# Strassen's seven products in the two feed-forward stages of a streaming encoder step, with the weight sums on GpSimd

## The chip, the cores and the metric

The kernel runs on one NeuronCore of a Trainium2 chip. TensorE (PE) multiplies matrices out of SBUF into PSUM; VectorE (DVE), ScalarE (ACT) and GpSimd (POOL) work elementwise, and GpSimd reaches SBUF alone; SyncE (SP) issues nearly all DMAs. The metric is the device time in microseconds of one execution, the median of several runs. Everything is in float32; lower is better.

## The reference, cut to what matters

Two layers are run over 1152 tokens (1024 of a prompt, 8 x 16 of samples) with a width of 1024. Each layer has a mixer and then the feed-forward stage that the change is about; 2816 is the stage's inner width:

```python
def conv_ffn(h, conv_hist, w_in, conv_w, conv_b, w_out):
    """(gelu(causal_dwconv(x W_a)) * x W_b) W_down."""
    T = h.shape[1]
    proj = jnp.einsum('btd,df->btf', h, w_in)              # 1024 -> 2 * 2816
    a, gate = proj[..., :D_FF], proj[..., D_FF:]
    full = jnp.concatenate([conv_hist.astype(a.dtype), a], axis=1)
    conv = conv_b + sum(full[:, j:j + T] * conv_w[j] for j in range(CONV_W))   # CONV_W = 3
    y = jnp.einsum('btf,fd->btd', jax.nn.gelu(conv, approximate=False) * gate, w_out)   # 2816 -> 1024
    return y, full[:, -(CONV_W - 1):].astype(conv_hist.dtype)

# per layer: x = x + mixer(rms_norm(x)); x = x + conv_ffn(rms_norm(x)); at the end y = rms_norm(x)
```

## The kernel before, in words

Activations lie transposed in SBUF: the width on the partitions (8 blocks of 128), the tokens along the free side. PE's fast float32 form rounds its operands, so every operand is kept in two parts, a high one (a rounded copy by ACT) and a low one (the remainder, a subtraction by DVE), and each product is three matmuls: high x high, high x low, low x high. In the names, `wh`/`wl` are the parts of a weight piece of 128x512, `xh`/`xl` of the activations, `yh`/`yl` of the inner activations.

A feed-forward stage goes in 11 steps over the inner width. In a step four units (`unit`, L707; its matmul is L723) make 2 x 128 inner channels of `a` and of the gate, each unit from 8 blocks of the width, 3 parts and 3 token blocks of 384: 72 matmuls of 128x384. DVE scales the result out of PSUM (L1417) and does the convolution (L1888 to L1900), ACT the gelu (L2610), GpSimd the product with the gate and its low part (L2977, L2983). Then `down` (L733, matmul L748, L772 for the last steps of layer 0) multiplies by 256 rows of `w_out`: 144 matmuls, which DVE adds to the residual `xs` (L1424). PE needs a step's inner activations only one step later, so its stream is never broken. The gain of the norm is multiplied into the weights by GpSimd (L2836), and 1/rms is applied when a result leaves PSUM. So a stage begins with activations that are not yet normed, while the norm is still being worked out: the squares by ACT, their sum by GpSimd (L2842), the sum over partitions by PE (L790), the root by ACT (L2215), the reciprocal by DVE (L1436).

Layer 0's stage is followed by the projection of the chunk mixer (`v` groups, L1246, 128x512 matmuls with the activations as the stationary operand). Layer 1's last two down steps are fused with the final norm and the output (`fin_part`, L1335, matmul L1353): PE turns the residual into rows beside them, so that only the last tile's norm and store come after the last matmul.

The order of the work is written out by hand, engine by engine, with semaphores between them; a table of counts (`PLAN`) numbers the weight pieces and the uses of the accumulator banks. One DMA queue (SP) loads the weights, 256 KB a piece, four pieces ahead.

## Time and profile before

| | us |
|---|---|
| median of 3 runs | 2838.18 |
| lowest and highest run | 2835.65, 2838.43 |
| the profiled execution: span from its first to its last instruction | 2835.0 |
| span less than the median | 3.2 |
| feed-forward stage of layer 0, to the first `v` matmul | 830.5 |
| feed-forward stage of layer 1, to the end | 845.2 |

The profile gives for each engine the time in which it was busy, the chain of work that ended last, and groups of instructions with their mean duration. A matmul's own duration overlaps that of the next; the spacing of a row of them is what counts. The stages are told apart by the line of their matmuls.

### The profile page before, as it was taken

The numbers are of one execution on the slowest core, as the hardware profiler recorded it, in microseconds if no ns is written. First come the engines' busy times: TensorE is split into PE (matmuls) and PEld (weight loads), VectorE is DVE, ScalarE is ACT, GpSimd is POOL, SyncE is SP. The second block draws the span as 40 slices with busy tenths as digits, with TensorE's granted clock in tenths as the row PEclk, the third lists the DMA queues.
The fourth block names the chain that finished last, engine by engine and source line by source line (L and its number), as shares of the span: only waits on it lengthen the run. The fifth ranks groups of instructions, "written<-read, shape, count | busy, mean of one in ns | idle before, by whom it ended". The sixth has DMA issues, their size and how long they took to land.

```text
span 2835.0 us, 44317 instructions
## 1 busy us (share of the span) xinstructions
PE 2809.9 (99%) x16164; PEld 2735.6 (96%) x16164; DVE 1477.7 (52%) x2678; ACT 707.6 (25%) x1191; POOL 733.5 (26%) x540
## 2 busy tenths in 40 slices
PE   9999999999999999999999999999999999999999
PEld 9999999999999999999888999999999999999997
DVE  3658975554444444457323755556544444444454
ACT  4424463211111111114222221214211111111114
POOL 3233325322222222223001230013422222222220
PEclk9999999999999999999999999999999999999999
DMA  4111001111111111111211111111111111111112
GB/s 146 41 43 40 24 27 48 41 42 41 44 41 41 42 43 41 41 45 45 60 51 58 34 42 41 44 41 34 52 42 41 44 41 41 44 41 41 44 48 85
DMA packets 195026, 130.70 MB, mean 46 GB/s; under 512 B 8876, under 2 KB 186741, under 8 KB 194677
## 3 DMA queue, kind: packets, MB, share of 16 engines
q1 hardware_dynamic: 194900, 129.43, 15.2%
q8 instruction: 61, 1.00, 0.1%
q14 instruction: 33, 0.26, 0.0%
q10 hardware_dynamic: 32, 0.01, 0.0%
HBM read 120.60 MB, written 8.81 MB: 46 GB/s over the span
## 4 chain that ended last, share of the span: by engine, by line
PE 94%; DVE 4%; issue 1%; ACT 1%; DMA 0%; POOL 0%; DVEq 0%; SPq 0%; ACTq 0%; POOLq 0%
PE bank L723 49%; PE bank L748 21%; PE bank L1246 7%; PE bank L772 3%; PE bank L884 3%; PE bank L1170 2%; PE bank L1353 2%; PE bank L919 1%; PE bank L822 1%; PE bank L1306 1%; DVE qsc L1548 1%; DVE work L2050 0%; PE bank L1138 0%; DVE sct L1569 0%; PE bank L905 0%
## 5 line engine op out<-in xcount | busy, mean ns | idle before, releaser
L2836 POOL TENSOR_TENSOR raw<-raw,vec 128x512 f32<-128x512 f32 x248 | 279.5, 1138 | 1297.2 <-DMA raw<-in_w_in_ffn 844.3
L723 PE MATMUL bank<-xh,wh 128*128 128x384 f32 x2664 | 607.2, 335 | 0.7 <-issue 0.7
L723 PE MATMUL bank<-xl,wh 128*128 128x384 f32 x2664 | 604.5, 334 | 0.0
L723 PE MATMUL bank<-xh,wl 128*128 128x384 f32 x2664 | 604.4, 334 | 0.0
L2181 ACT ACTIVATE wh<-raw 128x512 fp32r<-128x512 f32 x374 | 235.3, 629 | 1396.3 <-PE bank L723 781.1
L1398 DVE TENSOR_TENSOR wl<-raw,wh 128x512 fp32r<-128x512 f32 x374 | 283.7, 759 | 424.9 <-ACT wh L2181 424.9
L723 PEld LDWEIGHTS bank<-xh,wh 128*128 128x128 f32 x2664 | 473.6, 188 | 2.8 <-issue 1.5
L723 PEld LDWEIGHTS bank<-xl,wh 128*128 128x128 f32 x2664 | 474.6, 188 | 0.0
L723 PEld LDWEIGHTS bank<-xh,wl 128*128 128x128 f32 x2664 | 474.4, 188 | 0.0
L1424 DVE TENSOR_TENSOR xs<-bank,xs 128x384 f32<-128x384 f32 (+1 forms) x648 | 320.9, 550 | 280.3 <-PE bank L748 246.8
L748 PE MATMUL bank<-yh,wh 128*128 128x384 f32 x1152 | 265.0, 338 | 0.0
L748 PE MATMUL bank<-yl,wh 128*128 128x384 f32 x1152 | 264.9, 338 | 0.0
L748 PE MATMUL bank<-yh,wl 128*128 128x384 f32 x1152 | 264.8, 338 | 0.0
L748 PEld LDWEIGHTS bank<-yh,wl 128*128 128x128 f32 x1152 | 207.4, 188 | 0.0
L748 PEld LDWEIGHTS bank<-yh,wh 128*128 128x128 f32 x1152 | 207.3, 188 | 0.0
L748 PEld LDWEIGHTS bank<-yl,wh 128*128 128x128 f32 x1152 | 207.2, 188 | 0.0
L2977 POOL TENSOR_TENSOR gate<-gate,cv 128x1152 f32<-128x1152 f32 x40 | 115.5, 2887 | 233.5 <-DVE xs L1424 211.7
L1417 DVE TENSOR_TENSOR gate<-bank,rstd 128x384 f32<-128x384 f32 x132 | 65.4, 550 | 178.9 <-PE bank L723 178.9
L1417 DVE TENSOR_TENSOR apad<-bank,rstd 128x384 f32<-128x384 f32 x88 | 45.0, 553 | 137.4 <-PE bank L723 137.4
L2983 POOL TENSOR_TENSOR yl<-gate,yh 128x1152 fp32r<-128x1152 f32 x40 | 114.7, 2885 | 0.0
L2610 ACT ACTIVATE cv<-cv 128x1152 f32<-128x1152 f32 x44 | 51.4, 1168 | 248.3 <-DVE cv L1895 248.3
L1892 DVE SCALAR_TENSOR_TENSOR cv<-apad,convc,cv 128x1024 f32<-128x1024 f32 x88 | 112.2, 1275 | 0.0
(340 smaller groups left out, 3369.6 us busy)
## 6 DMA issues: line engine op xcount, KB each, us to landing
raw<-in_w_in_ffn SPq DMA_DIRECT2D x176, 256.0 KB, 2.9
raw<-in_w_out_ffn SPq DMA_DIRECT2D x88, 256.0 KB, 2.7
raw<-in_w_uv_c SPq DMA_DIRECT2D x64, 256.0 KB, 2.8
raw<-in_w_in_ab SPq DMA_DIRECT2D x40, 256.0 KB, 2.9
raw<-in_w_out_c SPq DMA_DIRECT2D x32, 256.0 KB, 2.7
xtok<-in_x_prompt SPq DMA_DIRECT2D x8, 512.0 KB, 7.7
raw<-in_w_out_ab SPq DMA_DIRECT2D x16, 256.0 KB, 2.7
out_y_prompt<-otok SPq DMA_DIRECT2D x8, 512.0 KB, 2.6
```

The lines of the kernel that those rows point to most:

```text
L723: mm = pe.matmul(ps[(sg + tb) % BANKS][:, 0:TB], w[:, place, k * P:(k + 1) * P], r[:, kk, tbs(tb)], start=kk == 0 and c == 0, stop=kk == K ...
L748: mm = pe.matmul(ps[(sg + g0 + tb) % BANKS][:, 0:TB], w[:, place, k * 256 + dd * P:k * 256 + (dd + 1) * P], r[:, k, tbs(tb)], start=k == 0 ...
L772: mm = pe.matmul(ps[(g0 + tb) % BANKS][:, 0:TB], w[:, a, k * 256 + dd * P:k * 256 + (dd + 1) * P], r[:, k, tbs(tb)], start=first, stop=last)
L1246: mm = pe.matmul(ps[g % BANKS][:, :], x[:, k, t * P:(t + 1) * P], w, start=k == 0 and e == 0, stop=k == KD - 1 and e == 2)
L1398: dve.tensor_tensor(wl[:, s % 2, :], raw[:, s % RAWS, :], wh[:, s % 2, :].bitcast(F32), ALU.subtract)\
L1417: dve.tensor_tensor(dst, ps[bank % BANKS][:, 0:TB], rstd[:, tbs(tb)], ALU.mult)\
L1424: dve.tensor_tensor(xs[:, d, tbs(tb)], ps[sg % BANKS][:, 0:TB], xs[:, d, tbs(tb)], ALU.add)\
L1892: dve.scalar_tensor_tensor(outp, padp[:, j:j + SEQ], col(16 + j), outp, ALU.mult, ALU.add)\
L2181: act.activation(wh[:, s % 2, :], raw[:, s % RAWS, :], ACT.Copy).then_inc(w_high_ready, 1)
L2836: pool.tensor_tensor(r, r, g, ALU.mult).then_inc(w_scaled, 1)
L2977: pool.tensor_tensor(gate[:, c, :], gate[:, c, :], cv[:, c, :], ALU.mult)\
L2983: pool.tensor_tensor(yl[:, c, :], gate[:, c, :], yh[:, c, :].bitcast(F32), ALU.subtract)\
```

## The change

Both feed-forward stages are written anew; the rest is touched only where the stages meet it.

Each of the two multiplications is seen as two by two blocks times two by two blocks: the width in halves of 512, the inner channels in pairs of 128-blocks (up) or the output width in halves (down), the tokens in halves of 576. Strassen's scheme makes the four result blocks from seven block products, not eight, each of a sum of weight blocks and a sum of activation blocks; the results are added up afterwards. Every operand still has a high and a low part.

**Up.** 22 pairs of 128-blocks, 7 products each. A product is 4 blocks of the half width x 3 parts x 2 chunks of 288 tokens: 24 matmuls of 128x288 (L1391 in the new file), into one double bank. The activations are normed first, in place (`normed`, by DVE), and the seven sums of them are formed once in a stage (`combos`) and kept with their parts in 28 tiles of 2 x 576. The four sums of weights of a pair are formed by GpSimd (`first_sums`, `up_sum`) from unscaled weights. ACT and DVE take each product out of PSUM and combine it with saved ones (`up_evict`).

**Room.** The 28 tiles need the room of the residual and of the inner activations. So the residual `xs` goes to a scratch tensor in DRAM before it is normed, and comes back in the down part; the inner activations `y` are stored to DRAM too, 2 blocks a step, and are read back in four blocks.

**Down.** 7 products of 11 steps; a step is 4 output blocks x 3 parts x 2 chunks: 24 matmuls (L1423) again. GpSimd forms the sums of weights (`w_sum`, 5 of the 7 products) and of `y` (`y_sum`, 5 of the 7, of which 3 are the same); parts lie in rings of 4 steps. The first two and the last two steps of a product are run as pairs, output block by output block. After each product DVE adds its four results to the residual (`down_evict`).

**Ends.** The stage of layer 0 ends with the high and low parts of the new residual, which the `v` groups wait for (`finished`, after the last step). The fused end of layer 1 is gone: after the last step PE turns the tiles, then square, root, reciprocal, product with the gain and store follow per tile (`finish`).

```diff
@@ the plan
-    PLAN.add(f"f{_l}0", 8, 12, 16)
-    PLAN.add(f"f{_l}", 9 * 12, 9 * 36, 9 * 40)
-    PLAN.add(f"f{_l}u", 8, 12, 16)
+HT = TOK // 2
+CH = HT // 2
+PAIRS = 2 * STEPS
+UPS = 7 * PAIRS
+DOWNS = 7 * STEPS
+RING = 3
+RINGD = 4
+        UP_ORDER = (1, 6, 2, 7, 5, 4, 3)
+        DOWN_ORDER = (2, 1, 5, 3, 6, 4, 7)
+        SUMMED_W, SUMMED_Y = (2, 1, 5, 6, 7), (1, 3, 6, 4, 7)
@@ SP
+                for d in range(KD):
+                    sp.wait_ge(acc_free, g0 + NTB * (d + 1))
+                    sp.dma_start(xscr[l][d], xs[:, d, :]).then_inc(x_moved, 16)
...
+                store_y(STEPS - 1)
+                step_weights(8)
+                sp.wait_ge(y_saved[0], 16 * 12 * (l + 1))
+                y_tiles(yb22[:, 9:11, :], 20, 22, T2S, y_back[2])
+                for d in range(0, KD, 4):
+                    sp.dma_start(xs[:, d:d + 4, :], xscr[l][d:d + 4].rearrange("d p t -> p d t")).then_inc(x_moved, 16)
@@ PE
+                def product(n, j):
...
+                    pe.wait_ge(f_high, done + pos + 1)
+                    pe.wait_ge(f_low, done + pos + 1)
...
+                    for k in range(4):
+                        if n == 0:
+                            pe.wait_ge(c_high, (28 + DOWNS) * l + 4 * j + k + 1)
+                            pe.wait_ge(c_low, (28 + DOWNS) * l + 4 * j + k + 1)
+                        x, _, m = combo(j, k)
+                        for e, (w, part) in enumerate(((fh, 0), (fh, 1), (fl, 0))):
+                            for c in range(2):
+                                mm = pe.matmul(bank[:, M0 + c * CH:M0 + (c + 1) * CH], w[:, pos % RING, k * P:(k + 1) * P],
+                                               x[:, m, part, c * CH:(c + 1) * CH], start=first and k == 0 and e == 0,
+                                               stop=k == 3 and e == 2, skip_group_check=True)
+                    mm.then_inc(f_done, 1)
...
+                for j in range(7):
+                    r0 = STEPS * j
+                    for first, last in ((0, 2), *((k, k + 1) for k in range(2, STEPS - 2)), (STEPS - 2, STEPS)):
+                        for f in range(4):
+                            for kk in range(first, last):
+                                down_step(r0 + kk, f)
@@ DVE, the start of a stage
+                for pos in range(RING):
+                    up_low(pos)
+                inv_rms(1 + 2 * l)
+                dve.wait_ge(x_moved, 160 * l + 16 * KD)
+                for d in range(4):
+                    normed(d, T1S)
+                for k in range(4):
+                    combo_low(0, k)
+                for k in range(4):
+                    normed(k, T2S)
+                    normed(4 + k, T2S)
+                    normed(4 + k, T1S)
+                    combos(k)
+                    combo_low(1, k)
...
+                for pos in range(1, UPS):
+                    if 2 <= pos < 7:
+                        for k in range(4):
+                            combo_low(pos, k)
+                    up_evict(pos - 1)
+                    convs(pos)
+                    if pos + 2 < UPS:
+                        up_low(pos + 2)
@@ GpSimd, the down part
+                def w_sum(r):
...
+                    pool.wait_ge(raw_loaded[ra], va)
+                    pool.wait_ge(raw_loaded[rb], vb)
+                    ring_free(r)
+                    pool.tensor_tensor(ring(r)[2], fraw[:, ra, :], fraw[:, rb, :],
+                                      ALU.subtract if q in (6, 7) else ALU.add).then_inc(f_summed, 1)
...
+                    pool.wait_ge(f_done, done + UPS + r - 3)
+                    pool.tensor_tensor(yslf[:, r % RINGD, :], y_block(a, kk), y_block(b, kk),
+                                       ALU.subtract if q in (3, 4) else ALU.add).then_inc(ys_summed, 1)
...
+                for r in range(4, DOWNS):
+                    w_sum(r)
+                    y_sum(r)
+                    j, kk = divmod(r, STEPS)
+                    if l == 0 and j == 6 and 4 <= kk <= 9:
+                        for m in (2 * kk - 8, 2 * kk - 7):
+                            add_square(24 * 2 + m, m % 2, m % NTB, sq_b, ssq_b)
@@ ACT, the end of layer 0's stage
+            def finished(d):
+                act.wait_ge(d_out, 24 + d + 1 if d < 4 else 20 + d - 3)
+                act.activation(xh[:, d, :], xs[:, d, :], ACT.Copy).then_inc(xh_ready, NTB)
```

DVE at the start of the first feed-forward stage: before, three low parts of weights and the reciprocals, then at once the scaling of results (`apad`, `cv` are the convolution's tiles).

```order
L1860 MEMSET apad 128x2 x2
L1398 TENSOR_TENSOR wl<-raw,wh 128x512 x3
L1436 RECIPROCAL rstd<-rstd 128x384 x3
L1417 TENSOR_TENSOR apad<-bank,rstd 128x384 x2
L1870 TENSOR_TENSOR apad<-bank,rstd 128x256
L1871 TENSOR_TENSOR apad<-bank,rstd 128x8x16
L1875 TENSOR_SCALAR apad<-convc 128x8x2
```

And in the changed kernel, behind the same reciprocals, the last of four such blocks and what comes next (`cw`, `cx` hold the activation sums, `fl` low parts of weights, `u_`, `p_` saved products).

```order
L2011 SCALAR_TENSOR_TENSOR xs<-xs,vec,rstd 128x576 x3
L2022 TENSOR_TENSOR cxf<-xs 128x576
L2024 TENSOR_TENSOR cxf<-xs 128x576
L2026 TENSOR_TENSOR cwf<-xs,cxf 128x576
L2029 TENSOR_TENSOR cxf<-xs,cwf 128x576
L2038 TENSOR_TENSOR cw<-cwf,cw 128x576
L2172 MEMSET apad_a 128x2
L2173 MEMSET apad_b 128x2
L2008 TENSOR_TENSOR fl<-flf,fh 128x512
L2038 TENSOR_TENSOR cw<-xs,cw 128x576 x4
L2053 TENSOR_TENSOR u_100<-bank,p_102 128x576
```

Norming and 16 sums now stand on DVE ahead of the second product's operands.

GpSimd around the end of the first feed-forward stage, before: gate product and low part, then the last weights to scale, then the squares' sums.

```order
L2836 TENSOR_TENSOR raw<-raw,vec 128x512 x3
L2977 TENSOR_TENSOR gate<-gate,cv 128x1152 x2
L2983 TENSOR_TENSOR yl<-gate,yh 128x1152 x2
L2836 TENSOR_TENSOR raw<-raw,vec 128x512 x5
L3010 MEMSET ssq_b 128x1152
L2842 TENSOR_TENSOR ssq_b<-ssq_b,sq_b 128x384 x24
```

And in the changed kernel's down part, product 6 of the first stage (`flf` sums of weights, `yslf` sums of `y`).

```order
L3281 TENSOR_TENSOR flf_113<-fraw 128x512
L3311 TENSOR_TENSOR yslf<-yb_119,yb_121 128x576
L3281 TENSOR_TENSOR flf<-fraw 128x512
L3311 TENSOR_TENSOR yslf<-yb_119,yb_121 128x576
L3281 TENSOR_TENSOR flf<-fraw 128x512
```

Each step of such a product now has two sums on GpSimd in front of its ACT and DVE parts.

## Rows read from the trace of the kernel before

**Rows 1.** The page: span, then engines' busy time.

```profile
span 2835.0 us, 44317 instructions
PE 2809.9 (99%) x16164; PEld 2735.6 (96%) x16164; DVE 1477.7 (52%) x2678; ACT 707.6 (25%) x1191; POOL 733.5 (26%) x540
```

**Rows 2.** The chain of waits: start us, us, what.

```profile
509.26 12.49 PE bank L723 x72
...
612.22 25.35 PE bank L748 x144
637.56 49.92 PE bank L723 x288
...
1481.16 65.33 PE bank L1246 x288
...
1989.78 6.24 PE bank L723 x36
```

**Rows 3.** Timeline of PE at layer 0's end: start us, us, engine, line, what.

```profile
1339.78 0.39 PE L1246 MATMUL bank<-wh,xh 128*128 128x512 f32 x1
```

**Rows 4.** Chain of waits after it.

```profile
1361.60 38.57 PE bank L1246 x170
```

**Rows 5.** Timeline of DVE in a step.

```profile
651.68 0.68 DVE L1398 TENSOR_TENSOR wl<-raw,wh 128x512 fp32r<-128x512 f32 x1
652.29 0.80 DVE L1888 TENSOR_SCALAR cv<-apad,convc 128x1024 f32<-128x1024 f32 x1
...
653.27 1.27 DVE L1892 SCALAR_TENSOR_TENSOR cv<-apad,convc,cv 128x1024 f32<-128x1024 f32 x1
654.47 0.34 DVE L1895 SCALAR_TENSOR_TENSOR cv<-apad,convc,cv 128x128 f32<-128x128 f32 x1
```

**Rows 6.** Timeline, layer 0's last down steps; brackets: idle before, and its releaser.

```profile
1299.71 0.55 DVE L1424 TENSOR_TENSOR xs<-bank,xs 128x384 f32<-128x384 f32 x1
1300.17 1.49 DVE L1430 TENSOR_TENSOR xl<-xs,xh 128x384 fp32r<-128x384 f32 x3
1301.31 7.77 POOL L2842 TENSOR_TENSOR ssq_b<-ssq_b,sq_b 128x384 f32<-128x384 f32 x6 [41.23 <-ACT sq_b L2208]
...
1304.26 3.96 DVE L1430 TENSOR_TENSOR xl<-xs,xh 128x384 fp32r<-128x384 f32 x3
```

**Rows 7.** Timeline of GpSimd: products and sums of 1152 and 512 columns.

```profile
635.74 2.69 POOL L2977 TENSOR_TENSOR gate<-gate,cv 128x1152 f32<-128x1152 f32 x1 [11.35 <-DVE xs L1424]
...
1573.13 5.16 POOL L3048 TENSOR_TENSOR gbc<-gbc,bbc 128x512 f32<-128x512 f32 x4
```

**Rows 8.** Timeline of the first stage's start.

```profile
509.15 1.49 DVE L1424 TENSOR_TENSOR xs<-bank,xs 128x384 f32 x3 [1.49 <-PE bank L1170]
510.87 3.68 POOL L2842 TENSOR_TENSOR ssq_e<-ssq_e,sq_e 128x384 f32<-128x384 f32 x3 [2.34 <-ACT sq_e L2208]
525.28 0.58 ACT L2215 ACTIVATE rstd<-bank,vec 128x384 f32<-128x384 f32 x1 [1.63 <-PE bank L790]
523.12 7.37 DVE L1436 RECIPROCAL rstd<-rstd 128x384 f32<-128x384 f32 x3
```

**Rows 9.** Instructions grouped by line: ACT copies, 512 and 1152 wide.

```profile
L2181 ACT ACTIVATE wh<-raw 128x512 fp32r<-128x512 f32 x374 | 235.3, 629 | 1396.3 <-PE bank L723 781.1 <-PE bank L748 524.8 <-PE bank L1170 34.4
L2606 ACT ACTIVATE yh<-gate 128x1152 fp32r<-128x1152 f32 x44 | 51.4, 1168 | 57.4 <-POOL gate L2977 51.8 <-DVE gate L1908 5.5
```

**Rows 10.** By stretch: us, busy (count) per engine, PEclk, DMA share, GB/s.

```profile
0.00:20.00 20.00, 15.07 (x75) 14.00 (x76) 7.71 (x14) 9.22 (x20) 11.54 (x28) 1.00 0.93 316
160.00:164.00 4.00, 4.00 (x17) 4.00 (x17) 0.00 (x0) 0.38 (x1) 2.97 (x3) 0.57 0.00 0
```

**Rows 11.** Timeline of the last tile.

```profile
2827.33 1.05 PE L1362 MATMUL bank<-ident,xs 128*128 128x128 f32 x8
...
2829.81 0.60 ACT L2803 ACTIVATE fin_sq<-bank 128x512 f32<-128x512 f32 x1 [2.65 <-PE bank L1353]
...
2831.12 1.41 DVE L2170 SCALAR_TENSOR_TENSOR otok<-bank,fin_sums,fin_gain 128x512 f32<-128x512 f32 x2
```

**Rows 12.** The page: DMA issues, KB each, us to landing.

```profile
raw<-in_w_out_ffn SPq DMA_DIRECT2D x88, 256.0 KB, 2.7
out_y_prompt<-otok SPq DMA_DIRECT2D x8, 512.0 KB, 2.6
```

More of the change, by code:

```diff
@@ new lines, in build, with up_slot, formed, combo @@
+        LOADS0 = tuple(STEPS * sum(len(DOWN_LOADS[q]) for q in DOWN_ORDER[:j]) for j in range(7))
+        def up_slot(n, q):
+            return psp[(3 * n + UP_SLOT[q]) % 4]
+        def formed(l, k, which):
+            return 32 * l + 4 + 7 * k + which + 1
+        def combo(x, k):
+            m = 4 * x + k
+            return (cw, cwf, m) if m < 12 else (cx, cxf, m - 12)
+        FFN_LOADS = STEPS + (LOADS0[6] + 2 * STEPS + 7) // 8
+        def loads_before(l, s):
+            return (PIECES if l else V_N) // RAWS + FFN_LOADS * l if s < RAWS else (FFN_LOADS - 1) * l
@@ new lines, in ring, with y_block, up_sums, sums_of @@
+        def ring(r):
+            e = (3, 1, 2, 0)[r % 4]
+            return (fh3[:, :], fl3[:, :], flf3[:, :]) if e == 3 else (fh[:, e, :], fl[:, e, :], flf[:, e, :])
+        def y_block(b, kk):
+            if b == 21 and kk == STEPS - 1:
+                return yb21_last[:, :]
+            return {11: yb11, 12: yb12, 21: yb21, 22: yb22}[b][:, kk, :]
+        def up_sums(l, n, which):
+            return (4 * PAIRS + len(SUMMED_W) * STEPS) * l + 4 * n + which + 1
+        def sums_of(r, which):
+            j, kk = divmod(r, STEPS)
+            return STEPS * sum(q in which for q in DOWN_ORDER[:j]) + kk + 1
@@ new lines, in build, with on_dve, on_act, dest @@
+        U2, U3, C22, C21, C12 = range(5)
+        P1, C11 = range(2)
+        def on_dve(l, n, which):
+            return 5 * (PAIRS * l + n) + which + 1
+        def on_act(l, n, which):
+            return 2 * (PAIRS * l + n) + which + 1
+        def dest(n, c, h):
+            if n % 2:
+                return ((gate[:, c, (T1S, T2S)[h]], slice(0, HT)),)
+            padp, pads = pads_of(c)
+            if h == 0:
+                return ((padp[:, 2:2 + HT], slice(0, HT)),)
+            return ((padp[:, 2 + HT:2 + SEQ], slice(0, SEQ - HT)), (pads[:, :, 2:], slice(SEQ - HT, HT)))
@@ L1393, in _ @@
+            for t in range(NT):
+                finish(t)
         @block.vector
@@ L1815, in abo @@
                         low(n0 + 4 * i + 2 * u + 1, n0 + 2 * u + 1)
-                    if not first or u:
+                    if (not first or u) and not (last and u):
                         low(n0 + 4 * i + 2 * u + 2, n0 + 2 * u + 2)
@@ L2461, in gate_silu @@
                 act.wait_ge(acc_free, g0 + 3 * (16 + h) + 3)
-                act.activation(work[:, 12 + h, :], work[:, 12 + h, :], ACT.Silu).then_inc(g_act, 1)
+                act.activation(work[:, 12 + h, :], work[:, 12 + h, :], ACT.Silu).then_inc(q_act, 1)
             def head_high(h):
@@ L2554, in _, with abo @@
             n0, g0, t0 = PLAN.at["abo"]
-            def abo(i):
-                first = isinstance(i, int)
+            def abo(i, first=False, last=False):
                 for u in range(2):
-                    if not first or u:
+                    if (not first or u) and not (last and u):
                         for p, tk in ((2, 1), (3, 4)):
@@ new lines, in ffn @@
+                for pos in range(RING):
+                    up_high(pos)
+                rms(1 + 2 * l)
+                for x in range(2):
+                    for k in range(4):
+                        combo_high(x, k)
+                act.wait_ge(convc_mm, 1 + l)
+                act.activation(convc[:, :], ps[7][:, 0:440], ACT.Copy).then_inc(convc_ready, 1)
+                for pos in range(1, UPS):
+                    n, j = divmod(pos, 7)
+                    if pos < 6:
+                        for k in range(4):
+                            combo_high(pos + 1, k)
+                    up_evict(pos - 1)
+                    if pos + 2 < UPS:
+                        up_high(pos + 2)
+                    else:
+                        w_high(pos + 2 - UPS)
+                        y_high(pos + 2 - UPS)
+                    if n % 2 and j == 5:
+                        gelu(n // 2, 0)
+                    if n % 2 == 0 and n and j == 2:
+                        gelu(n // 2 - 1, 1)
@@ L3002, in ffn @@
[L3002 to L3016 removed]
+                done = PER * l
@@ new lines, in ffn @@
+                if l == 0:
+                    pool.wait_ge(states_stored, 16 * (1 + HEADS))
+                up_sum(1)
+                for pos in range(3, UPS):
+                    up_sum(pos)
+                    n, j = divmod(pos - 2, 7)
+                    if n and n % 2 == 0 and j in (0, 4):
+                        y_prod(n // 2 - 1, j // 4)
+                w_sum(0)
+                w_sum(1)
+                y_prod(STEPS - 1, 0)
+                w_sum(2)
+                w_sum(3)
+                y_prod(STEPS - 1, 1)
```

1222 lines of the change are left out of this document (671 added, 551 removed).

## The prediction

> **What bounds the kernel now.** I read the page's shares first: PE is busy for 2809.9 of 2835.0 us, the others for half of it or less [rows 1]. The chain of waits then shows two patterns that alternate through both feed-forward stages: 288 matmuls of a step's four units in 49.92 us and 144 of its down part in 25.35 us [rows 2], one behind the other without a gap. That is 173.3 and 176.0 ns per matmul of 384 columns. Nothing but PE bounds these stages, so fewer or shorter matmuls are worth their whole time, until another engine can no longer keep up. Fewer columns go through PE after the change (7 of 8 products), but the other engines get much more to do, so the question is where PE will wait.
>
> Stage of layer 0: from 509.26 [rows 2] to the first `v` matmul at 1339.78 [rows 3], 830.5 us. Stage of layer 1: from 1989.78 [rows 2] to 2835.0, 845.2 us.
>
> **PE's part.** No row has a stream of matmuls of 288 columns. The `v` groups' 288 matmuls of 512 columns take 65.33 us [rows 2], 226.8 ns each; against 173.3 for 384 columns that is 53.5 ns for 128 columns, 0.418 ns a column, with 13.3 ns fixed. So 288 columns: 120.4 + 13.3 = 133.7 ns, with the ends 120 (nothing fixed) and 173.3 (no shorter than 384). I take 133.5, a product or a down step of 24 is 3.20 us, and 3.23 with what a change of group costs. A layer has 22 x 7 = 154 products and 7 x 11 = 77 down steps: 231 x 3.23 = 746 us. By PE alone the change would save 84 us in layer 0 and 99 in layer 1.
>
> **A stage's start.** Before, PE begins at once on activations that are not normed; now all 28 activation sums wait for the norm. Before the first product: the last residual sums (1.49), squares, their sums on GpSimd (3.68 for three), the root (0.58), the reciprocals (7.37) [rows 8]; some overlap, about 13 us. `normed` also waits for the residual's eight stores of 590 KB to the scratch tensor: 4.7 MB at the 316 GB/s of the kernel's fastest stretch [rows 10] is 15 us, started while the norm is worked out, so it hides nearly all of itself. Then DVE norms 16 tiles (8 blocks in two halves), forms 16 sums and takes 28 low parts, 60 operations of 576 columns. A DVE operation with two inputs takes 0.61 us for 512 columns and 1.20 for 1024, from one start to the next [rows 5]: 0.68 for 576. With 0.73 for the norming ones, 42 us; the evictions, `fl` parts and first copies among them add 6, and PE at a lower clock after its pause 2 to 3 (such a stretch exists: PEclk 0.57 with short, scattered matmuls [rows 10]). ACT's 28 copies of 576 columns lie between 629 and 1168 ns each [rows 9], 0.68 by their width, 19 us in all, beside DVE. Pair 0 ends about 64 us after the stage's start; its PE work is 7 x 3.23 = 22.6. Loss: 41 us a layer. Bounds: 28 (the stores, evictions and half the norm hidden) and 50 (sums slowed by GpSimd).
>
> **The up part.** For 14 products (two pairs, 45.2 us on PE) GpSimd has 8 weight sums of 512 columns and two gate products of 1152. It takes 5.16/4 = 1.29 us for 512 and 2.69 for 1152 columns [rows 7]; 8 x 1.2 + 2 x 2.69 = 15 us. DVE has some 25: evictions, low parts, two convolutions at about 4.3. Even if they excluded each other the 40 us fit under 45.2, so I let the remaining 147 products go at PE's pace: 475 us. If this cover fails by a tenth, it costs 20 us or more a layer.
>
> **Up to down.** The last convolution, gate product, high and low part and the first sums follow one another: 4.3 + 2.7 + 1.2 + 2.4 us and PE has two pairs' products of margin for a part of it only. I take 11 us, bounds 2 and 18.
>
> **The down part.** 77 x 3.23 = 249 us. In products 1, 6 and 7 (33 steps) GpSimd forms both a weight sum (512) and a `y` sum (576), and DVE takes the low part of each. What these cost together stands in the rows of the squares' sums: alone, three DVE low parts of 384 columns take 1.49 us; beside six GpSimd sums in 7.77 us, 3.96 us for three [rows 6]. One of each then takes 7.77/6 to 3.96/3, 1.30 to 1.32 us, where one DVE operation alone takes 0.50 and a GpSimd one 0.90 (2.69 us x 384/1152, [rows 7]): nearly their sum, so they exclude each other. 1.32/384 is 3.44 ns a column; 1088 columns give 3.74 us a step against PE's 3.23. 33 x 0.51 = 17 us a layer. Ends: 0 (they overlap; GpSimd's 1088 columns alone are 2.6 us) and 50 (each waits for the other's hand-over too). The rings are four steps deep, which covers a step or two, not eleven. The other four products have one such sum or none and stay under 3.23.
>
> The Trainium skill ("SBUF — State Buffer", the section on SBUF's two separate sides) says that GpSimd and VectorE share a port pair that one holds for a whole instruction, and that only VectorE operations with two SBUF inputs or a fast copy mode need it. [Rows 6] agree: the low parts, with two SBUF inputs, are held up, and L1424's sum out of PSUM takes its 0.55. By that rule the evictions here would go free, as I assume.
>
> **Small stalls.** Evictions between products, and SP's queue: the residual's return (4.7 MB, 15 us by [rows 10]) and `y`'s reads stand in front of weight pieces that otherwise land in 2.7 us [rows 12]. 8 us a layer, between 0 and 25.
>
> **Only in layer 0.** Twelve squares' sums stand in GpSimd's product 7, 0.9 us each as above: 10 us where GpSimd and DVE are already the limit. Then `v`. Before, it begins inside the stage and runs without gaps from 1361.60 [rows 4], 21.8 us after its first matmul. Now `xh`, `xl` and the squares of the last four blocks all follow the last steps: four evictions, copies and low parts at 2 us a block, six squares' sums at 1.1, norm and reciprocals as before. 36 us; 14 lost (bounds 5 and 25).
>
> **Only in layer 1.** After the last step: an eviction (0.68), eight transposes (1.05), squares (two of 0.60), root and reciprocal, the product with the gain (1.41) [rows 11], a store (2.6, [rows 12]) make 8 us with the hand-overs; eight more tiles share two output buffers: (1.41 + 2.6)/2 = 2.0 each. 24 us.
>
> **Sum.** 64 + 475 + 11 + 249 + 17 + 8 = 824, less 1 of rounding up: 823. Layer 0: 823 + 10 = 833, + 14 at `v`, against 830.5: +16. Layer 1: 823 + 24 = 847 against 845.2: +1.5. The span becomes 2835.0 + 17.5 = 2852.5; the median lies 3.2 above the span, so 2855 us.
>
> **Rivals.**
>
> A, the forecast: 0.55. Its own range is 2830 to 2880.
>
> B, GpSimd and DVE don't hold each other up in the down part as they do in [rows 6] (there a chain through two buffers of squares could have set the pace as well). Then the 34 us of heavy steps, the 10 of squares and some 10 of the hand-overs come back: 2801 us. For it: GpSimd alone needs 2.6 of 3.23 us. Against it: the low part's 0.50 became 1.32 beside running GpSimd work, which no buffer explains. 0.27.
>
> C, it comes out clearly slower by one mechanism: in products 1, 6 and 7 sum, copy and low part pass from GpSimd to ACT and DVE, and the ring's release comes back from PE three or four steps later. If exclusion and these waits add up to 4.5 us a step, 66 steps lose another 0.76 each, 50 us: 2905. It decides from about 3.9 us a step upwards. 0.11.
>
> D, PE's waits in these steps lower its clock. [Rows 10] show 0.57 of full speed in a stretch of scattered matmuls. At 1.2 GHz a step's 24 x 120 ns double; four fifths of that, 2.3 us in 66 steps, make 152 us: 3007. Against it: a wait here is a fraction of a microsecond between dense steps, not such a stretch. 0.04.
>
> E, the shorter matmul isn't cheaper: at 173.3 ns as for 384 columns, 11,088 matmuls x 40 ns = 443 us, about 3300. 0.03. [Rows 2] speak against it, since 512 to 384 columns follows a line nearly through zero.
>
> The Trainium skill ("TensorE: Matmul & The Clock Gate", Part 3, on the mechanism) lets a weight load overlap a running matmul only in another row group; by its 107 ns for a load, estimated, a matmul would take 120 + 107 = 227 ns and the change cost a millisecond more. [Rows 2] refute it for this kernel: 384 columns are 160 ns of columns and come every 173.3.
>
> **Numbers.** Two executions of this kernel can't be told apart below about 0.2%, here 2832.5 to 2843.9. Of A, 0.05 lies below, 0.12 within, 0.38 above. Faster: 0.05 + 0.27 = 0.32; same 0.12; slower 0.38 + 0.11 + 0.04 + 0.03 = 0.56. For 8 in 10 the range takes in B almost wholly and half of C: 2785 to 2905, with about 0.05 left below and 0.13 above.
>
> **What would show it.** The spacing of the new matmuls (133 ns; 3.23 us a product). The first product 13 to 17 us after the stage's start and pair 0's end at 64. In the down part 3.7 us a step in products 1, 6, 7 and 3.23 in the others, with DVE's low parts and GpSimd's sums never beside each other at full speed. A pause of about 11 us between up and down, `v` undisturbed 36 us after the last step, 24 us behind the last matmul. I am wrong if the up part runs slower than PE (DVE or GpSimd over 3.2 us a product), if the start costs 50 or more, or if the heavy steps run at 3.23.

## The result, and the profile after

The changed kernel takes 2871.6 us (median of 4 runs, 2869.6 to 2874.2) against 2837.5 of before (4 runs): ratio 1.0122, 95% interval 1.0108 to 1.0137. It is slower by 34 us. The forecast was slower, 2855 us; the direction was right and the size half of it. Its profiled span is 2867.9 us, 32.9 more than before's.

The page of the changed kernel: its span, then busy time by engine, as in [rows 1], and the clock in 40 slices.

```profile
span 2867.9 us, 45432 instructions
...
PE 2682.9 (94%) x17812; PEld 2595.6 (91%) x17812; DVE 1882.1 (66%) x2649; ACT 932.6 (33%) x1536; POOL 1056.8 (37%) x724
...
PEclk9999999699999998999999999999699999998999
```

PE's busy time fell by 127 us, and 127 + 33 = 160 us more of the span are now idle. DVE gained 404 us of work and GpSimd 323.

The long undisturbed stretch answers to [rows 2]. The chain of waits, layer 1's up part:

```profile
2082.30 467.82 PE bank L1391 x3528
```

467.82 / 3528 is 132.6 ns for a matmul of 288 columns; 133.5 was forecast from the line through 384 and 512 columns. Apart from pair 0 the up part runs at PE's pace without a gap, in both layers.

The two stages, term by term. "Measured" is read from the timeline of PE: the starts of every 24th matmul of L1391 and L1423 (264 make a down product).

| term, us | predicted | layer 0 | layer 1 |
|---|---|---|---|
| start of stage to the end of pair 0 | 64 | 72.9 | 73.2 |
| the other 147 products | 475 | 467.6 | 467.6 |
| pause between up and down | 11 | 7.0 | 7.0 |
| 77 down steps at PE's pace | 249 | 244.3 | 244.3 |
| lost in products 1, 6, 7 (two sums a step) | 17 | 16.6 | 16.6 |
| lost in product 2 (and the rest) | 8 | 18.3 | 21.8 |
| squares' sums in product 7 | 10 | 13.0 | |
| **to the last down matmul** | 833 / 823 | **839.7** | **830.5** |
| entry of `v`, or tail | 36 / 24 | 37.2 | 25.1 |

Before, the stages were 830.5 + 21.8 (entry of `v`) and 845.2, so these lines are 24.6 and 10.4 us more; 2 us less elsewhere make up the 32.9. Two lines of the table are a split and not a reading: layer 0's product 7 lost 16.7 us as a whole; 3.7 of it, as much as in layer 1, stand under the two sums a step, the other 13.0 under the squares' sums.

Stretches of the changed kernel: start of layer 0's stage, pair 0, the rest of the up part, product 2, product 1. Columns as in [rows 10].

```profile
507.00:528.00 21.00, 5.07 (x10) 1.91 (x8) 14.64 (x15) 7.43 (x13) 5.97 (x5) 0.59 0.51 180
528.00:554.00 26.00, 10.14 (x47) 9.03 (x48) 25.19 (x37) 3.96 (x7) 2.28 (x1) 0.63 0.00 0
554.00:580.00 26.00, 19.93 (x124) 18.58 (x124) 22.90 (x31) 15.19 (x27) 5.12 (x3) 0.85 0.14 42
580.00:1045.00 465.00, 465.00 (x3511) 464.23 (x3510) 336.11 (x463) 141.44 (x211) 182.51 (x104) 1.00 0.24 74
...
1055.00:1108.00 53.00, 40.81 (x266) 39.96 (x267) 28.87 (x32) 14.83 (x27) 21.78 (x13) 0.82 0.94 345
1108.00:1148.00 40.00, 36.92 (x261) 36.00 (x260) 37.44 (x30) 14.29 (x22) 34.23 (x21) 0.96 0.61 205
```

Four kinds of stretch read differently. In pair 0 DVE is busy for 48.1 of 52 us (third pair of numbers) while PE is busy for 30 (first pair); from 580 on PE is full and DVE at 72%; in product 2 the last two numbers stand out, the DMA engines at 94% and 345 GB/s; in product 1 DVE and GpSimd are both near full, 37.4 and 34.2 of 40 us.

What PE waited for in the down part of layer 0: the first matmul behind a wait, in brackets how long and on what.

```profile
1096.70 0.82 PE L1423 MATMUL bank<-ysh,fh 128*128 128x288 f32 x2 [10.37 <-ACT fh L2874]
1100.25 0.82 PE L1423 MATMUL bank<-ysh,fh 128*128 128x288 f32 x2 [1.77 <-ACT fh L2874]
...
1137.68 0.50 PE L1423 MATMUL bank<-ysh,fh 128*128 128x288 f32 x2 [0.18 <-ACT fh L2874]
1141.24 0.50 PE L1423 MATMUL bank<-ysh,fh 128*128 128x288 f32 x2 [2.52 <-ACT fh L2874]
```

The 10.4 us stand before step 9 (13.8 in layer 1); the prediction had 8 us for all small stalls together. The 2.5 us at the end of product 1 stand inside the two-step pair. By the order of the work it needs both its steps' parts, and so takes the slack of the ring at once; no run changes this order.

The waits are not the whole loss. Behind the 2.5 us the matmuls come in twos every 0.48 us, not every 0.27, and the granted clock is 0.50, the lower of TensorE's two levels (timeline, then a stretch with columns as in [rows 10]):

```profile
1143.10 0.68 PE L1423 MATMUL bank<-ysh,fl 128*128 128x288 f32 x2
1143.58 0.68 PE L1423 MATMUL bank<-ysh,fh 128*128 128x288 f32 x2
...
1142.20:1145.40 3.20, 3.20 (x15) 3.20 (x15) 3.20 (x6) 1.20 (x2) 0.03 (x1) 0.50 1.02 365
```

So product 1's 5.7 us are 3.1 of waits, 1.9 of slower matmuls and some smaller delays; product 6's 7.2 are 3.2 and 3.3. Of product 2's 17.9 us in layer 0, 5.2 are slower matmuls, behind the pause between up and down and behind the one before step 9; of product 7's 16.7 there, 5.0 are (0.6 in layer 1).

GpSimd in such steps (layer 1, product 1), and DVE beside it:

```profile
2641.96 1.94 POOL L3311 TENSOR_TENSOR yslf<-yb,yb 128x576 f32<-128x576 f32 x1
2643.86 1.73 POOL L3281 TENSOR_TENSOR flf<-fraw 128x512 f32<-128x512 f32 x1
2645.55 1.93 POOL L3311 TENSOR_TENSOR yslf<-yb,yb 128x576 f32<-128x576 f32 x1
```

```profile
2642.69 1.75 DVE L2125 TENSOR_TENSOR fl<-flf,fh 128x512 fp32r<-128x512 f32 x1
2644.64 1.56 DVE L2133 TENSOR_TENSOR ysl<-yslf,ysh 128x576 fp32r<-128x576 f32 x1 [0.20 <-ACT ysh L2892]
```

A sum follows a sum without a pause: 3.59 us a step (2641.96 to 2645.55), against PE's 3.18. The prediction had 3.74. Each DVE operation takes more than twice the 0.69 and 0.75 us that it takes alone.

### The profile page after: what moved, and what is told of

Read it like the earlier page. It is cut to its first block, busy times and chain, and to the rows that moved or that the text cites. A ratio compares the mean times of both kernels' runs of the same rounds, so it can differ in the third digit from the quotient of the medians.

```text
span 2867.9 us, 45432 instructions
## 1 busy us (share of the span) xinstructions
PE 2682.9 (94%) x17812; PEld 2595.6 (91%) x17812; DVE 1882.1 (66%) x2649; ACT 932.6 (33%) x1536; POOL 1056.8 (37%) x724
## 4 chain that ended last, share of the span: by engine, by line
PE 43%; POOL 3%; issue 2%; DVE 2%; DMA 1%; SPq 1%; ACT 0%; POOLq 0%; DVEq 0%; ACTq 0%
PE bank L1391 16%; PE bank L889 7%; PE bank L1459 6%; PE bank L914 5%; PE bank L1423 5%; PE bank L938 2%; POOL yslf L3311 1%; POOL flf L3281 1%; PE bank L1518 1%; DVE work L2284 0%; DMA y_scratch<-gate 0%; SPq L758 0%; DMA out_y_prompt<-otok 0%; DMA fraw<-in_w_out_ffn 0%; DVE otok L2392 0%
## 5 line engine op out<-in xcount | busy, mean ns | idle before, releaser
L1391 PE MATMUL bank<-cx,fh 128*128 128x288 f32 x2816 | 487.3, 294 | 7.0 <-DVE cx L2038 6.2
L1391 PE MATMUL bank<-cw,fh 128*128 128x288 f32 x2112 | 375.4, 300 | 56.3 <-DVE cw L2038 36.8
L1391 PEld LDWEIGHTS bank<-cx,fh 128*128 128x128 f32 x2816 | 411.8, 188 | 9.1 <-issue 8.0
L1391 PEld LDWEIGHTS bank<-cw,fh 128*128 128x128 f32 x2112 | 315.6, 192 | 62.7 <-issue 34.2
L1423 PE MATMUL bank<-ysh,fh 128*128 128x288 f32 x1232 | 275.8, 306 | 54.0 <-ACT fh L2874 35.6
L1391 PE MATMUL bank<-cx,fl 128*128 128x288 f32 x1408 | 298.8, 294 | 0.0
L1423 PE MATMUL bank<-ysh,fl 128*128 128x288 f32 x1232 | 271.2, 302 | 0.0
L1423 PE MATMUL bank<-ysl,fh 128*128 128x288 f32 x1232 | 270.3, 302 | 0.0
L1423 PEld LDWEIGHTS bank<-ysh,fh 128*128 128x128 f32 x1232 | 204.7, 196 | 63.4 <-ACT fh L2874 41.4
L1391 PE MATMUL bank<-cw,fl 128*128 128x288 f32 x1056 | 227.7, 298 | 0.0
L1391 PEld LDWEIGHTS bank<-cx,fl 128*128 128x128 f32 x1408 | 224.6, 187 | 0.0
L1423 PEld LDWEIGHTS bank<-ysl,fh 128*128 128x128 f32 x1232 | 205.6, 196 | 0.0
L1423 PEld LDWEIGHTS bank<-ysh,fl 128*128 128x128 f32 x1232 | 204.9, 195 | 0.0
L1391 PEld LDWEIGHTS bank<-cw,fl 128*128 128x128 f32 x1056 | 172.1, 191 | 0.0
```

What stands on the lines that cost most here:

```text
L1391: mm = pe.matmul(bank[:, M0 + c * CH:M0 + (c + 1) * CH], w[:, pos % RING, k * P:(k + 1) * P], x[:, m, part, c * CH:(c + 1) * CH], start=fi ...
L1423: mm = pe.matmul(psp[f][:, M0 + c * CH:M0 + (c + 1) * CH], w[:, f * P:(f + 1) * P], x[:, r % RINGD, c * CH:(c + 1) * CH], start=kk == 0 an ...
```

## The experiments

All are timed against the kernel before; ratios are to it, with their 95% interval, and the changed kernel stands at 1.0122. The first question was whether the pace of the heavy steps is set by exclusion (GpSimd and DVE on SBUF) or by the hand-over through ACT and the ring; the second, what bounds product 2; the third, whether the start is DVE's row of operations.

### e1: weights before the wait in SP's queue

```diff
-                step_weights(8)
+                for r in range(8, 12):
+                    step_weights(r)
                 sp.wait_ge(y_saved[0], 16 * 12 * (l + 1))
                 ...
-                for r in range(9, DOWNS):
+                for r in range(12, DOWNS):
```

> SP issues the weights of down steps 9 to 11 before it waits for the last inner activations to be stored, and before the residual's return. Theory (the one queue's order: step 9's weights stand behind a wait for a store, behind the rest of y, the residual and the conv tails): the pause of 10.4 us in layer 0 and 13.8 us in layer 1 before step 9's matmuls goes, and with it most of the 17.7 and 21.2 us that product 2 loses; 28 to 36 us in all, about 2840 us. Rival (the bytes are what takes the time, not their order: 4.7 MB of the residual and y come in one way or another): under 10 us, the pause moves to step 11 or to the first product's additions.

Measured: 2855.5 us, 1.0072 [1.0055, 1.0088], 16 us less than the change. Product 2 takes 45.8 and 47.4 us instead of 52.8 and 56.3. Neither side had the size. The pause before step 9 went, as the theory said, but as the rival said PE now waits at the first additions, which need the residual: 8.1 us, and 9.4 in layer 1. PE of this kernel, step 11:

```profile
1100.82 0.82 PE L1424 MATMUL bank<-ysh,fh 128*128 128x288 f32 x2 [8.12 <-DVE xs L2154]
```

### e5: half of the residual earlier

Product 2's additions need blocks 4 to 7 only, and their room is free during the up part.

```diff
                 step_weights(1)
+                sp.dma_start(xs[:, 4:8, :], xscr[l][4:8].rearrange("d p t -> p d t")).then_inc(x_half, 16)
...
-                for d in range(0, KD, 4):
-                    sp.dma_start(xs[:, d:d + 4, :], ...).then_inc(x_moved, 16)
+                sp.dma_start(xs[:, 0:4, :], ...).then_inc(x_moved, 16)
```

> As e1_queue, and the half of the residual that product 2's additions need (blocks 4 to 7, whose place is free) comes back already before the down part, the other half where it came before. After e1_queue product 2 still lost 10.7 and 12.3 us, of which PE waited 8.1 and 9.4 us for the first additions, and these for the residual. Theory (the residual's return is what is late): product 2 falls to 37 us or less in both layers, 16 us less than e1_queue, about 2840. Rival (the queue is short of time as a whole: what is brought earlier makes y or weights late): the pause moves to product 1 or before step 3, under 6 us gained.

Measured: 2848.3 us, 1.0044 [1.0030, 1.0058]; product 2 41.2 and 42.6 us. The median is 7 us under e1's and the profiled span 13; the intervals just meet, and the products' times show the 4.6 and 4.8 us gained here. That is less than expected but no shift: PE's wait for the first additions fell from 8.1 to 3.5 us (from 9.4 to 4.9 in layer 1). Together e1 and e5 take back about 12 of the 18 and 14 of the 21 us.

### e9: fewer bytes in product 2

Built on e8 (below). In e1 and e5 the DMA engines were busy for all of product 2, so I took bytes to be the floor. That stretch of e1 and of e5 (columns as in [rows 10]):

```profile
1055.00:1101.00 46.00, 37.79 (x265) 37.29 (x266) 24.90 (x28) 15.87 (x29) 23.87 (x14) 0.91 1.02 382
```

```profile
1056.00:1097.00 41.00, 37.68 (x264) 37.15 (x264) 23.75 (x27) 15.68 (x28) 23.70 (x14) 0.93 0.99 363
```

```diff
+                        n = 128 if 4 <= r < 12 else 512
-                        sp.dma_start(fraw[:, s, :]..., wfo[l][:, k:k + 1, fhalf * 512:(fhalf + 1) * 512])
+                        sp.dma_start(fraw[:, s, 0:n]..., wfo[l][:, k:k + 1, fhalf * 512:fhalf * 512 + n])
```

> e8_all with the weight pieces of down steps 4 to 11 loaded to 128 of their 512 columns (leaves out the rest of these loads: 3.1 MB a layer). In e8_all the DMA engines are busy for the whole of product 2, at 362 GB/s, and it takes 41.7 and 43.7 us instead of 35.1. Theory (product 2 is bound by bytes, after the order in the queue was mended): 3.1 MB at 362 GB/s are 8.7 us, so product 2 falls to 37 or 38 us in both layers, 8 to 11 us in all, about 2798. Rival (what is left are waits in the order of the work: the tails' way through ACT, the two-step pairs, the first additions): under 3 us.

Measured: 2804.0 us, 0.9884 [0.9867, 0.9900], beside 2810.0, 0.9901 [0.9884, 0.9918], of e8 on the same chip. The medians are 6 us apart and the intervals overlap. Product 2 took 40.7 and 42.5 us instead of 40.8 and 44.1, 1.7 us in all where 8 to 11 were expected; the other 4 us lie outside it and I can't assign them. The theory fell: once the order is mended, bytes no longer bound this product. Its stretches show what does (same columns):

```profile
1055.00:1060.00 5.00, 4.99 (x24) 4.44 (x23) 1.30 (x3) 0.45 (x1) 4.84 (x2) 0.65 0.70 196
1060.00:1065.00 5.00, 3.03 (x13) 3.03 (x13) 3.09 (x4) 2.94 (x8) 1.27 (x2) 0.69 0.76 236
1065.00:1070.00 5.00, 5.00 (x38) 5.00 (x38) 1.70 (x3) 2.32 (x4) 2.54 (x2) 0.96 1.03 372
1070.00:1090.00 20.00, 20.00 (x153) 20.00 (x152) 10.67 (x16) 7.44 (x13) 8.01 (x5) 1.00 0.70 254
```

In the timeline of PE the matmuls behind the pause between up and down, and again behind a wait of 2.0 us for the tails' bank, come in twos every 0.48 us, then every 0.27:

```profile
1061.97 0.85 PE L1427 MATMUL bank<-ysh,fh 128*128 128x288 f32 x2 [1.97 <-ACT trow L2833]
...
1064.06 0.68 PE L1427 MATMUL bank<-ysl,fh 128*128 128x288 f32 x2
1064.54 0.68 PE L1427 MATMUL bank<-ysh,fl 128*128 128x288 f32 x2
...
1065.97 0.43 PE L1427 MATMUL bank<-ysh,fh 128*128 128x288 f32 x2
1066.24 0.43 PE L1427 MATMUL bank<-ysl,fh 128*128 128x288 f32 x2
```

The granted clock there is 0.65 and 0.69, the lower of TensorE's two levels for part of the stretch. 2.0 us of waiting and 27 matmuls that together come 3.6 us late are 5.5 of the 5.8 us that layer 0's product 2 still loses. Layer 1's loses 7.6: 2.0 us at the same bank, 3.7 in slow matmuls, and 1.6 at the first additions, which wait for DVE:

```profile
2568.18 0.50 PE L1427 MATMUL bank<-ysh,fh 128*128 128x288 f32 x2 [1.57 <-DVE xs L2187]
```

### e2: all sums of the heavy steps on DVE

```diff
+                def dve_sums(r):
+                    ...
+                    dve.wait_ge(f_done, done + UPS + r - 3)
+                    if q in SUMMED_W: dve.tensor_tensor(ring(r)[2], fraw[:, ra, :], fraw[:, rb, :], ...)
+                    if q in SUMMED_Y: dve.tensor_tensor(yslf[:, r % RINGD, :], y_block(a, kk), y_block(b, kk), ...)
...
+                        dve_sums(r + 1)
                     w_low(r)
                     y_low(r)
```

> From the second down product on, DVE forms the sums of weights and of y, not GpSimd. Theory (GpSimd and DVE exclude each other; a step with two sums is 3.6 us of GpSimd time beside 3.19 of PE): DVE does two sums and two low parts in 2.55 us a step, with the evictions 33 of 35 us a product, so the waits of products 1, 6 and 7 (5.5, 7.0, 3.5 us a layer) nearly go; product 7 of layer 0, with the squares' sums still on GpSimd, falls from 51.4 to about 44 us. 32 to 40 us in all, about 2835. Rival (the hand-over from sum to high part to low part and the ring of four set the pace): no gain, or slower, since DVE now waits for PE twice a step: 2870 or more.

Measured: 2831.9 us, 0.9984 [0.9974, 0.9993]: 40 us less than the change, and just under the kernel before. Product 1 takes 34.9 us in both layers (40.6), product 6 35.7 (42.1), product 7 35.8 in layer 1 (38.6) and 42.7 in layer 0 (51.6). DVE in product 1:

```profile
1127.97 0.69 DVE L2149 TENSOR_TENSOR flf<-fraw 128x512 f32<-128x512 f32 x1 [0.54 <-PE bank L1423]
1128.58 0.75 DVE L2161 TENSOR_TENSOR yslf<-yb,yb 128x576 f32<-128x576 f32 x1
1129.25 0.69 DVE L2125 TENSOR_TENSOR fl<-flf,fh 128x512 fp32r<-128x512 f32 x1
1129.85 0.75 DVE L2133 TENSOR_TENSOR ysl<-yslf,ysh 128x576 fp32r<-128x576 f32 x1
```

Four operations in 2.6 us, where two of them took 3.3 beside GpSimd. DVE has twice the operations and is done sooner, and now even waits for PE.

### e3: no sums of weights, sums of y left on GpSimd

This takes work away and leaves the path from GpSimd to ACT to DVE and back from PE as it was.

```diff
-        SUMMED_W, SUMMED_Y = (2, 1, 5, 6, 7), (1, 3, 6, 4, 7)
+        SUMMED_W, SUMMED_Y = (2,), (1, 3, 6, 4, 7)
```

> Leaves out the sums of weights from the second down product on (the first of the two pieces is used as it is; both are loaded); the sums of y stay on GpSimd. Theory (exclusion): 1.43 us of GpSimd and 1.27 of DVE a step are 2.7, under PE's 3.19, so the waits of products 1, 6 and 7 go and layer 0's product 7 comes to 40 us or less: 35 to 43 us, about 2832. Rival (hand-over and ring: the y sum still goes from GpSimd to ACT to DVE and comes free by PE): the waits stay, under 10 us gained.

Measured: 2834.1 us, 0.9992 [0.9983, 1.0002]; products 1 and 6 34.9 us, product 7 42.2 and 35.1 (40 or less was expected of layer 0's, where the squares' sums are still on GpSimd). With e2 this settles it: the waits go when the sum of both engines' durations comes under PE's step, whether the sums of `y` stay on GpSimd (e3) or all go to DVE (e2). The way through ACT and the ring of four are there in both.

### e4: narrow norm

```diff
+                    few = slice(ts.start, ts.start + 32)
-                    dve.scalar_tensor_tensor(xs[:, d, ts], xs[:, d, ts], ..., rstd[:, ts], ALU.mult, ALU.mult)
+                    dve.scalar_tensor_tensor(xs[:, d, few], xs[:, d, few], ..., rstd[:, few], ALU.mult, ALU.mult)
```

> Norms 32 columns of each tile instead of 576 (leaves out the rest of the norm's product), 16 operations a layer. Theory (at a stage's start PE waits for DVE's row of operations and for nothing else, so each of them counts in full): 16 x 0.65 = 10.4 us a layer, 21 us in all, about 2851. Rival (ACT's copies, the weight sums on GpSimd or the scratch stores of the residual come next close behind): under 8 us in all.

Measured: 2853.0 us, 1.0062 [1.0046, 1.0079], 19 us less. From the stage's start to pair 0's end it is 64.4 us instead of 72.9 in layer 0, 65.4 instead of 73.2 in layer 1: 8.5 and 7.8 of the 10.4 us taken out.

### e11: narrow reciprocals

Built on e8.

```diff
+                    few = slice(tb * TB, tb * TB + (16 if k in (1, 3) else TB))
-                    dve.reciprocal(rstd[:, tbs(tb)], rstd[:, tbs(tb)]).then_inc(rstd_ready, 1)
+                    dve.reciprocal(rstd[:, few], rstd[:, few]).then_inc(rstd_ready, 1)
```

> e8_all with the reciprocals at the start of both stages taken over 16 of each 384 columns (leaves out the rest). Theory (the chain at a stage's start has no slack: the norm, then DVE's row): the last root comes 2 us after the first reciprocal begins, so 7.4 us of reciprocals become about 2.2: 5 us a stage, 10 in all, about 2798. Rival (the scratch stores of the residual, waited for right behind the reciprocals, are only just done by then and take their place): under 4 us.

Measured: 2797.9 us, 0.9861 [0.9844, 0.9877], 12 us under e8 on the same chip. The first product begins 14.7 and 15.7 us after the stage's start instead of 20.5 and 20.7. The scratch stores are no bound even then. Pair 0 ends 6.3 and 4.5 us earlier, measured from the stage's start as in e8. So every part of the chain at the start counts nearly in full.

### e10: narrow squares

Built on e8.

```diff
+                few = slice(tb * TB, tb * TB + (16 if 48 <= e < 60 else TB))
-                pool.tensor_tensor(ssq[:, tbs(tb)], ssq[:, tbs(tb)], sq[:, par, :], ALU.add)
+                pool.tensor_tensor(ssq[:, few], ssq[:, few], sq[:, par, 0:few.stop - few.start], ALU.add)
```

> e8_all with the twelve sums of squares that stand in layer 0's product 7 cut to 16 of 384 columns (leaves out the rest). Theory (they exclude DVE, which has 33 of 35 us of work there): product 7 of layer 0 falls from 42.6 to layer 1's 35.8 us: 7 us, about 2801. Rival (layer 0's product 7 waits for ACT's copies and squares, not for the sums): under 2 us.

Measured: 2800.6 us, 0.9876 [0.9859, 0.9892] against 0.9901; product 7 of layer 0 takes 35.8 us, exactly layer 1's, instead of 42.7. In the changed kernel itself the same twelve sums cost 13.0 us by the split above, 4.4 of them as slower matmuls.

### e6: GpSimd's order at the hand-over

```diff
                 y_prod(STEPS - 1, 0)
-                w_sum(2)
-                w_sum(3)
                 y_prod(STEPS - 1, 1)
+                w_sum(2)
+                w_sum(3)
```

> GpSimd forms the weight sums of down steps 2 and 3 after the last gate product, not before it. Theory (exclusion: in the trace these sums stand beside the last convolution, whose 1024-column operations take 3.7 and 2.3 us there against 1.3 alone): the convolution ends about 4 us earlier, and PE's pause of 7 us between up and down falls to 3 or 4: 6 to 8 us in all, about 2865. Rival (the sums of steps 2 and 3 then come too late, or the pause is set by the tails' way through PE and ACT): no gain, the pause stands before step 2.

Measured: 2871.5 us, 1.0124 [1.0107, 1.0141]: nothing. The second long operation of the convolution did fall from 2.28 to 1.27 us, and the pause between up and down from 7.0 to 5.0. But the 2 us came back one step later:

```profile
1062.70 0.53 PE L1423 MATMUL bank<-ysh,fh 128*128 128x288 f32 x2 [2.09 <-ACT trow L2796]
```

PE now waits for the bank from which ACT copies the convolution's tails. The rival's second half, the tails' way, was right.

### e7: four output buffers

```diff
-        otok = at("otok", [P, 2, D], F32, slot(20))
+        otok = at("otok", [P, 4, D], F32, slot(8))
...
-                if t >= 2:
-                    dve.wait_ge(y_stored[t % 2], 16 * (t // 2))
+                if t >= 4:
+                    dve.wait_ge(tile_sem[t % 4], tile_base[t % 4] + 16 * (t // 4))
```

> Four output buffers at the end instead of two. Theory (from the third tile on DVE waits for the store of the tile two before: 1.3 + 2.65 us for two tiles): the tail of 25 us falls to 20, set by ACT's two squares and root of 1.5 us a tile: 2866. Rival (the stores queue behind each other, or ACT paces the tiles already): under 2 us.

Measured: 2865.9 us, 1.0099 [1.0082, 1.0116]. That is 6 us under the change, though the intervals still touch; the profile shows the tail at 20.4 us instead of 25.1, with a tile every 1.54 us, ACT's square and root:

```profile
2848.66 1.03 ACT L3077 ACTIVATE fin_sq<-bank 128x1024 f32<-128x1024 f32 x1
...
2850.19 1.03 ACT L3077 ACTIVATE fin_sq<-bank 128x1024 f32<-128x1024 f32 x1
```

### e8: e2, e5, e6 and e7 together

> e2_dve_sums with the changes of e5_early_half, e6_handover and e7_tail. Theory: the parts lie in different places and add up: 2832 less 33 (product 2), 7 (hand-over) and 5 (tail): about 2787, 1.7% under the kernel before. Rival (DVE, with both sums and the evictions at 33 of 35 us a product, has no room left and gives the gain of product 2 back): 2805 or more.

Measured: 2807.9 us, 0.9901 [0.9885, 0.9918]; again, beside e9 to e11,

> The same kernel as e8_all, as the measure for the three beside it: 2808 us, 0.990 of the kernel before.

2810.0 us, 0.9901 [0.9884, 0.9918]. It leaves nothing out and is 28 us faster than the kernel before and 64 faster than the changed one. It is 21 us over its expectation: product 2 is 19 us shorter than in e2, not 33 (41.7 and 43.7 us), e6's part gave nothing, and product 1 rose from 34.9 to 36.4 us a layer, where DVE must now add product 2's results and form the sums at once; so the rival had a small part of it.

## Why the prediction was right, and where its size was off

**PE's part: right.** 133.5 ns was predicted for a matmul of 288 columns, 132.6 came. The line was read 0.5 ns too high: 173.3 less 384 x 0.418 leaves 12.8 fixed, not 13.3, so it gives 133.2. Rival E and the 227 ns worked out from a weight load are refuted for this kernel by the same row. Both parts ran at 3.18 us a step (22.27 for a pair's seven products), not at the 3.23 that allowed for waits at a change of group: 12 us a layer on the good side.

**Up part hidden: right, by another sum than the forecast's.** PE stayed full. But in 44.5 us of it (two pairs) GpSimd was busy for 17.5 us, not 15, and DVE for 32, not 25 (182.51 and 336.11 in the 465 us above). The 50 us together are more than PE's 44.5, so "even if they excluded each other" the work would fit doesn't hold for these durations, which contain the time held up. The margin was thinner than forecast.

**Heavy steps: right in mechanism, the size partly by luck.** 3.74 us a step was worked out from the squares' sums; 3.59 came, and the loss is 16.6 us a layer against 17. e2 and e3 show the mechanism; B and C fell. But 33 steps at 3.59 instead of 3.18 are 13.5 us, and of these the ring covers a part: in products 1 and 6 PE waits from step 7 on. In layer 1 the three products have 8.6 us of waits, and 5.8 us are slower matmuls behind the longest of them. That is rival D's mechanism, at 6 us a layer and not the 76 of its price, and the forecast's sum had no term for it here. The exclusion is not total: alone, the four operations would take 1.26 + 1.40 + 0.60 + 0.67 = 3.93 us.

The row that the prediction names for a sum out of PSUM (0.55 us at 1299.71, [rows 6]) ends before GpSimd's first sum at 1301.31, so it doesn't show what happens beside one; the changed kernel does.

The Trainium skill ("SBUF — State Buffer", on SBUF's two separate sides) has VectorE operations held up by GpSimd if they have two SBUF inputs or run in a mode that uses both of VectorE's ports, as a `tensor_scalar` can, and others not. The changed kernel's convolution agrees. GpSimd forms weight sums from 1041.55 on; beside them:

```profile
1041.77 0.76 DVE L2065 TENSOR_TENSOR gate<-bank,u 128x576 f32<-128x576 f32 x1 [0.40 <-PE bank L1391]
...
1042.79 1.84 DVE L2087 TENSOR_SCALAR cv<-apad_a,convc 128x1024 f32<-128x1024 f32 x1
```

The addition out of PSUM keeps its 0.76 us; the operation with one SBUF input and a fast rate (0.81 us at 581.39, where GpSimd is idle) takes 1.84.

**Squares in layer 0: right.** 10 predicted, 13.0 came (8.1 of waits, 4.4 of slower matmuls), and e10 takes 6.9 us out of e8 where GpSimd has nothing else there.

**The start: mis-sized.** "Pair 0 ends about 64 us after the stage's start" was 73. The sum had 13 for the norm's chain, 42 + 6 for DVE's row and 2 to 3 for a lower clock. Measured are 16.6 + 52.2 + 4.1 = 72.9.

The norm's chain took 16.6 us, not 13: the reciprocals end at 524.1, since PE's sums over the partitions, 2.9 us for the first two blocks, ACT's roots and the reciprocals follow one another. DVE's row starts there, not at 528, and has 52.2 us of work up to 580.4, not 48. The 4.2 us more are operations beside four sums of GpSimd. The same four low parts take 2.76 us alone and 4.93 beside two of them:

```profile
561.13 2.76 DVE L2038 TENSOR_TENSOR cx<-cxf,cx 128x576 fp32r<-128x576 f32 x4
570.06 4.93 DVE L2038 TENSOR_TENSOR cx<-cxf,cx 128x576 fp32r<-128x576 f32 x4
570.22 1.73 POOL L3239 TENSOR_TENSOR s1t<-fraw 128x512 f32<-128x512 f32 x1 [1.96 <-DVE fl L2008]
```

Four more (565.02) take 3.85, and one `combos` addition 1.64 instead of 0.76; together that is the 4.2. So the exclusion, used for the down part, was left out of the start. And DVE stood idle for 4.1 us, 3.0 of them waiting for one weight's high part, which ACT has queued behind the last activation sum's copy, four more copies of activations and a product out of PSUM. The term for the clock didn't add: DVE's row sets the time here, whatever PE's clock (0.63, then 0.85). e4 and e11 show that what is taken from either piece of this chain returns at three quarters or more. With both layers this is 18 of the missing us.

**Product 2: the failed step.** "8 us a layer, between 0 and 25" stood for all small stalls; they are 18.3 and 21.8. The price of the residual's return was right (4.7 MB, 15 us; 14.9 came from issue to landing in layer 0, 16.9 in layer 1). What I did not do is follow SP's queue in order, though the prediction named it: the weights of step 9 stand behind a wait for the last `y` store, and that store takes 11.5 us, where the median of such stores is 3.3: two reads of `y` and eight weight loads were issued in the 8 us before it (chain of waits, layer 1; start us, us, what):

```profile
2567.57 11.51 DMA y_scratch<-gate
...
2594.25 9.87 DMA fraw<-in_w_out_ffn
```

A piece that normally lands in 3 us takes 9.9 behind the residual. e1 and e5 move the weight loads of three steps and half of the residual, and take back two thirds. What e5 leaves, 6.2 and 7.7 us, is 3.5 and 4.9 of waiting for the first additions and 2.6 and 2.7 of slower matmuls.

**Hand-over: 7 us, 4 below the forecast.** e6 shows that the convolution's length is only one of two bounds, the tails' bank is the other.

**Entry of `v` and tail: right** (37.2 for 36; 25.1 for 24).

The terms of the sum give 16.5 + 1.8 = 18.3 us; 17.5 was carried on, by rounding. So the forecast's 17 us became 33: 18 more from the starts and 24 from product 2 (with what else is in that line of the table), less 24 from the faster steps and 8 from the hand-overs; the rest, about 5, is the squares (3), the entry of `v` and the tail (2) and rounding.

Where did PE's gain go? At 3.18 us a step, 231 steps take 735 us, 96 and 110 less than the two stages before: 206 us. Given back are 101 in the two starts (51 us each beyond the pair's own 22), 14 in the pauses between up and down, 40 in product 2, 33 in the heavy steps, 13 for the squares, 15 at `v` and 25 in the tail: 241.

## What to carry to other kernels

Before a scheme that trades matrix work for elementwise work, count the elementwise work that stands before the first matmul, not its share of the whole: the norm and 52 us of DVE work behind it cost 50 here, twice, while 336 us spread over the up part cost nothing. Two engines that hold each other up on SBUF are nearly one engine: add their durations (3.93 us for what took 3.59), and give the work to the faster one (DVE takes 0.60 us for what GpSimd takes 1.26). In a single DMA queue, read what each wait stands in front of; the weights of three steps moved ahead of one wait gave 16 us. And count a pause of PE with the slower matmuls behind it.
